# Top-2 experts of a decoder step: tokens fetched by indirect DMA in place of one-hot gathers

## Chip, cores and metric

The kernel runs on one core of a Trainium2 chip. The metric is the device time of one execution in microseconds (us), the median of several runs. The trace comes from one further, profiled execution.

## The reference

A two-layer decoder trunk runs one inference step on 320 tokens (256 of a prompt, 8 sequences of 8) with 1024 channels, in float32. Both layers mix tokens (pooling, convolution, gated DeltaNet) and end in a feed-forward part; layer 0 has a dense one, layer 1 has 8 experts of width 1408, of which each token uses two. Only the experts are touched here:

```
vals, idx = lax.top_k(xt @ w_router + b_router, 2)
gate = sum(one_hot(idx, 8) * softmax(vals)[..., None], axis=1)
for e in range(8):
    out = out + gate[:, e:e+1] * ((silu(xt @ wg[e]) * (xt @ wu[e])) @ wd[e])
```

## The kernel before

Precision is float32 throughout. Every matrix is split into a high part (`mh`, `xeh`, `hTh`: a copy rounded to the format TensorE multiplies) and a low part (`ml`, `xel`, `hTl`: the value minus its high part), and each product is three matmuls, low x high, high x low, high x high (L1340 to L1342, in `wide`).

**The expert stage** starts behind the router. A token's slot in its expert (`posm`) makes one-hot matrices `Pm` (`places`, VectorE, L1957), 128 slots for each expert. The first pair of experts gets its tokens by `gather`: matmuls of the token rows `xth` and `xtl` with `Pm` (L1288). Then the eight experts follow one another. An expert has 27 rows of weights, `MN`: 8 gate rows and 8 up rows of 1408 columns (704 KB each, 9 matmuls each, into banks 0 to 2 and 3 to 5), and 11 down rows of 1024 columns (512 KB, 6 matmuls, banks 6 and 7).

**A row's path**: SP loads it into one of 7 buffers `mraw` (L517), once the low part of the row 7 before is made; ScalarE copies it to one of 4 buffers `mh` (`mhead`, L901), once TensorE is through with the row 4 before; the low part `ml` is made by GpSimd for the rows in `MPOOL` (7 of the 27, L583) and by VectorE for the rest (`mlo`, L1938); then TensorE multiplies it. VectorE and ScalarE run step by step in the order of rows: step n makes row n + 3, and other work is placed behind it.

**Between up and down** ScalarE has put silu of the gate banks into `sg1`; VectorE multiplies it with banks 3 to 5 (L2012), TensorE transposes the product (11 transposes, L1389), ScalarE takes the high part `hTh` (L961) and VectorE the low part `hTl` (L2018). In experts 0 to 5 TensorE also gathers here for the expert two further on: 24 matmuls with `Pm`, half ahead of the transposes and half behind them (`gather_next`, for `xth` in even experts, for `xtl` in odd ones). Each gather ends in copies out of the banks on ScalarE and VectorE (`gathered`).

**Other work.** Even experts make the gates by slot (`slots`, L1306) and, from expert 2 on, add the pair before to the result: `scatter` (L1329, L1330) behind rows 3 to 10, whose banks VectorE adds to `acc` (`add`, L1977). Odd experts transpose `Pm` (`places_turned`). At an expert's end `y_head` (ScalarE) and `y_rest` (VectorE, L1972) take the down banks.

Of the kernel before, what the change touches and what calls it, by code (L numbers as in the profile page):

```python
# [54 lines left out]
MPOOL = (3, 6, 9, 12, 19, 22, 25)  # L55
# [11 lines left out]
for _n, _w in (("ident", 128), ("ones", 1), ("pick", 15), ("cum_p", 128), ("blk_p", 128), ("strict_p", 128), ("cum_s", 64),  # L67
               ("blk_s", 64), ("strict_s", 64), ("ind_p", 8), ("ind_s", 8), ("lev", 6 * 128), ("lev0t", 128),
               ("invcnt", 64), ("before", 64),
               ("upto", 128), ("slot", 128)):  # L70
    CON[_n] = (_at, _w)
    _at += _w
# [3 lines left out]
def build(nc, io):  # L76
# [8 lines left out]
    with ctx:  # L85
# [6 lines left out]
        def lay(at, *plan):  # L92
# [10 lines left out]
         gslot, flag, warm, TOP) = lay(  # L103
# [12 lines left out]
            ("gslot", [128, NE], f32), ("flag", [128, 1], mybir.dt.int32), ("warm", [1, 1], f32))  # L116
# [49 lines left out]
        assert E7 <= XS + 2 * size([1, KT, T]) + 12 * UNIT * 4  # L166

# [65 lines left out]
        m_hi, m_lop, m_lod, m_done = sem("m_hi"), sem("m_lop"), sem("m_lod"), sem("m_done")  # L233
        m_p, m_pt, m_ptc, m_gs = sem("m_p"), sem("m_pt"), sem("m_ptc"), sem("m_gs")
# [110 lines left out]
        def pooled(n):  # L345
            return n % MN in MPOOL

        def m_rest(n):

            mine = pooled(n)  # L350
            return (m_lop if mine else m_lod), sum(pooled(v) == mine for v in range(n + 1))
# [177 lines left out]
        def _(pool):  # L529
# [26 lines left out]

            pool.sem_inc(f_lo, 5)
            for l in range(DEPTH):
# [18 lines left out]
                else:  # L577
                    for n in range(MT):
                        if not pooled(n):
                            continue  # L580
                        w = mwidth(n % MN)
                        pool.wait_ge(m_hi, n + 1)
                        pool.tensor_tensor(ml[:, n % MS, 0:w], mraw[:, n % MRAW, 0:w],  # L583
                                           mh[:, n % MS, 0:w].bitcast(f32), ALU.subtract).then_inc(m_lop, 1)
# [8 lines left out]
        def _(act):  # L593
# [309 lines left out]
            def experts():  # L903
# [17 lines left out]
                def gathered(e, n):  # L921

                    act.wait_ge(m_g, 8 + 4 * e + n + 1)
                    dst = xel[:, 2 * n:2 * n + 2, :] if e % 2 else xeh[:, (e // 2 + 1) % 2, 2 * n:2 * n + 2, :]
                    act.activation(dst, PS[(7, 6, 0, 1)[n]][:, :].rearrange("p (k n) -> p k n", k=2), ACT.Copy)\
                        .then_inc(m_xea, 1)
# [10 lines left out]
                for n in range(MT):  # L937
# [3 lines left out]
                    if n and n + 3 < MT:  # L941
                        mhead(n + 3)
                    if i == MG - 1:
# [4 lines left out]
                    if i == 4 and e % 2 == 0:  # L948
                        act.wait_ge(m_gs, e // 2 + 1)
                        act.activation(gslot[:, e:e + 2], PS[3][:, 0:2], ACT.Copy).then_inc(m_ptc, 1)  # L950
# [4 lines left out]
                    if i == MG + MU - 1:  # L955
                        if e < NE - 2:
                            gathered(e, 0)
# [6 lines left out]
                        if e < NE - 2:  # L964
                            gathered(e, 2)
# [51 lines left out]
        def _(pe):  # L1017
# [253 lines left out]
            def experts():  # L1271
# [21 lines left out]
                def gather_next(e, n):  # L1293

                    gather(PS[(7, 6, 0, 1)[n]], xtl if e % 2 else xth, e // 2 + 1, n)

                def slots(e):

                    if e:
                        pe.wait_ge(m_tlo, 3 * e)  # L1300
                    pe.wait_ge(m_p, e + 2)
                    if not e:
                        pe.wait_ge(gate_made, 1)
                    for j in range(2):
                        for t in range(3):
                            ins = pe.matmul(PS[3][:, j:j + 1], Pm[0:rows(t), e // 2 % 2, t, j, :].bitcast(f32),  # L1306
                                            gate[0:rows(t), t, e + j:e + j + 1], start=(t == 0), stop=(t == 2))
                    ins.then_inc(m_gs, 1)
# [10 lines left out]
                def scatter(pair, m):  # L1319

                    if m == 0:
                        pe.wait_ge(m_ylo, 4 * pair + 4)
                        pe.wait_ge(m_ptc, 3 * pair + 3)
# [20 lines left out]

                pe.wait_ge(m_p, 2)
# [5 lines left out]
                for e in range(NE):  # L1351
# [7 lines left out]
                    def fed(k):  # L1359
                        return xeh[:, e // 2 % 2, k, h], xel[:, k, h]  # L1360

                    for k in range(8 + SCAT):
                        if k < MG:
                            wide(e * MN + k, PS[0:3], FUNIT, *fed(k), k == 0, k == MG - 1)
                        else:
                            if k == MG:
                                pe.wait_ge(m_ptc, 3 * (e // 2) + (3 if e % 2 else 1))
                            wide(e * MN + k, PS[3:6], FUNIT, *fed(k - MG), k == MG, False)
                        if k == 2:
                            if e % 2:  # L1370
                                places_turned(e)
                            else:
                                slots(e)
# [3 lines left out]
                    for k in range(SCAT, MU):  # L1377
                        wide(e * MN + MG + k, PS[3:6], FUNIT, *fed(k), False, k == MU - 1)

                    if e < NE - 2:  # L1380
                        pe.wait_ge(m_p, 2 * (e // 2) + 4)
                        pe.wait_ge(m_ylo, 2 * e)
                        pe.wait_ge(m_acc, 8 * (e // 2))
                        gather_next(e, 0)
                        gather_next(e, 1)
                    for c in range(3):
                        pe.wait_ge(m_h, e * 3 + (c + 1))
# [4 lines left out]
                    if e < NE - 2:  # L1392
                        pe.wait_ge(m_silu, e * 3 + 3)
                        gather_next(e, 2)
                        gather_next(e, 3)
                        pe.wait_ge(m_xea, XA0 + 2 * e + 1)
                        pe.wait_ge(m_xev, XV0 + 2 * e + 1)
                    else:
                        pe.wait_ge(m_ylo, 2 * e)
                        pe.wait_ge(m_acc, 8 * (e // 2))  # L1400
# [61 lines left out]
        def _(dve):  # L1462
# [470 lines left out]
            def mlo(n):  # L1933
                if pooled(n):
                    return
# [3 lines left out]
                                  mh[:, n % MS, 0:w].bitcast(f32), ALU.subtract).then_inc(m_lod, 1)  # L1939

            def experts(l):
# [3 lines left out]
                dve.memset(gate[:, :, NE:], 0.0)  # L1945
# [15 lines left out]
                def gathered(e, n):  # L1961

                    dve.wait_ge(m_g, 8 + 4 * e + n + 1)
                    dst = xel[:, 2 * n:2 * n + 2, :] if e % 2 else xeh[:, (e // 2 + 1) % 2, 2 * n:2 * n + 2, :]
                    dve.tensor_copy(dst, PS[(7, 6, 0, 1)[n]][:, :].rearrange("p (k n) -> p k n", k=2)).then_inc(m_xev, 1)
# [28 lines left out]
                for n in range(MT):  # L1994
# [3 lines left out]
                    if n + 3 < MT:  # L1998
# [3 lines left out]
                    if i in (5, 7) and e % 2 == 0 and e < NE - 2:  # L2002
                        if e:
                            dve.wait_ge(m_pt, e // 2)
                        places(e + 2 + (i - 5) // 2)
                    if i == MG + MU - 1:
                        dve.wait_ge(m_silu, e * 3 + 3)
                        dve.wait_ge(m_done, e * MN + MG + MU)
                        for c in range(3):
                            w = min(512, FUNIT - 512 * c)  # L2010
                            s = slice(512 * c, 512 * c + w)
                            dve.tensor_tensor(sg1[:, s], sg1[:, s], PS[3 + c][:, 0:w], ALU.mult).then_inc(m_h, 1)  # L2012
                        if e < NE - 2:
                            gathered(e, 1)
                        for c in range(3):
                            k = min(4, FT - 4 * c)
# [4 lines left out]
                        if e < NE - 2:  # L2021
                            gathered(e, 3)
# [72 lines left out]
def _constants():  # L2095
# [22 lines left out]
    put("upto", (i <= j).astype(np.float32))  # L2118
# [102 lines left out]
```

## Time and profile before

| | |
|---|---|
| median of 3 runs | 1652.11 us (1652.07 to 1652.57) |
| profiled execution | 1651.5 us, its span 1649.7 us |
| mean granted TensorE clock | 0.948 of 2.4 GHz |
| busy over the span | TensorE 92%, VectorE 65%, ScalarE 52%, GpSimd 34% |
| expert loop | from 1166.95 us to about 1617 us of the span |

The span reaches from the first to the last instruction; the time of an execution is 1.8 us longer. A busy share is an average over stages that have different limits. Only the last third of the span, the experts, is touched by the change.

### The profile page before, as it was taken

What the parts mean: (1) busy time and instruction counts of PE and PEld (TensorE: products, weight loads), DVE (VectorE), ACT (ScalarE), POOL (GpSimd) and SP (SyncE); (2) the same over time, 40 slices, a digit from 0 to 9 for tenths busy, and PEclk for the clock granted to TensorE, in tenths of its full rate; (3) what the DMA queues carried; (4) which work ended last, traced back from release to release, by engine and by line L of the source; (5) the groups of instructions that cost most, each with busy time, mean ns of one, the idle gap of its engine ahead of it and who ended that gap; (6) DMA issues with size and microseconds to landing.
All of it is one profiled execution on the core that took longest, in us unless ns stands there. A gap on an engine that the chain in (4) does not pass through costs nothing. (4 is left out here: it accounts for less than half of the span.)

```text
span 1649.7 us, 23014 instructions
## 1 busy us (share of the span) xinstructions
PE 1520.7 (92%) x8707; PEld 1339.8 (81%) x8707; DVE 1077.6 (65%) x1546; ACT 853.0 (52%) x1472; POOL 555.4 (34%) x336
## 2 busy tenths in 40 slices
PE   7999799999799999799998998996999999999995
PEld 6789799787699999678898988973788888888774
DVE  6779786658611011467887855777477877787784
ACT  4656555532433233355565635313566676576673
POOL 0036543000376567300555520010233343343342
PEclk9999899989899999999998998897799999999998
DMA  6322124312355455053322333125387987798780
GB/s 245 128 77 92 63 77 133 128 52 96 128 165 167 118 152 166 1 182 103 103 78 77 100 118 120 55 80 206 126 302 284 330 314 289 256 358 319 266 328 33
DMA packets 57523, 264.66 MB, mean 160 GB/s; under 512 B 9024, under 2 KB 9664, under 8 KB 48448
## 3 DMA queue, kind: packets, MB, share of 16 engines
q1 hardware_dynamic: 57408, 263.11, 45.9%
q8 instruction: 74, 1.21, 0.3%
q14 instruction: 41, 0.34, 0.1%
HBM read 254.54 MB, written 8.54 MB: 159 GB/s over the span
## 5 line engine op out<-in xcount | busy, mean ns | idle before, releaser
L1020 PE MATMUL ps<-Xh,Wl 128*128 128x320 f32 x976 | 332.0, 340 | 26.2 <-DVE Wl L1816 14.6
L1938 DVE TENSOR_TENSOR ml<-mraw,mh 128x1408 fp32r<-128x1408 f32 (+1 forms) x160 | 291.4, 1854 | 75.9 <-ACT mh L901 75.9
L901 ACT ACTIVATE mh<-mraw 128x1408 fp32r<-128x1408 f32 (+1 forms) x216 | 268.0, 1253 | 112.9 <-PE ps L1342 110.9
L1021 PE MATMUL ps<-Xl,Wh 128*128 128x320 f32 x976 | 312.9, 321 | 0.0
L1022 PE MATMUL ps<-Xh,Wh 128*128 128x320 f32 x976 | 312.7, 320 | 0.0
L555 POOL TENSOR_TENSOR cacc<-cacc,G 128x320 f32<-128x320 f32 x180 | 192.5, 1069 | 350.4 <-ACT G L681 334.3
L583 POOL TENSOR_TENSOR ml<-mraw,mh 128x1408 fp32r<-128x1408 f32 (+1 forms) x56 | 178.7, 3192 | 320.3 <-ACT mh L901 320.3
L1020 PEld LDWEIGHTS ps<-Xh,Wl 128*128 128x128 f32 x976 | 193.9, 199 | 50.4 <-issue 29.2
L1816 DVE TENSOR_TENSOR Wl<-raw,Wh 128x1024 fp32r<-128x1024 f32 x138 | 174.9, 1268 | 75.9 <-ACT Wh L610 74.9
L1021 PEld LDWEIGHTS ps<-Xl,Wh 128*128 128x128 f32 x976 | 194.4, 199 | 0.3
L1022 PEld LDWEIGHTS ps<-Xh,Wh 128*128 128x128 f32 x976 | 193.6, 198 | 0.0
L535 POOL TENSOR_TENSOR fl<-fraw,fh 128x1024 fp32r<-128x1024 f32 (+1 forms) x60 | 158.6, 2649 | 88.4 <-ACT fh L848 88.4
L610 ACT ACTIVATE Wh<-raw 128x1024 fp32r<-128x1024 f32 x138 | 144.9, 1052 | 46.0 <-PE ps L1022 37.7
L1340 PE MATMUL ps<-mh,xel 128*128 128x512 f32 (+1 forms) x384 | 147.0, 383 | 1.9 <-issue 0.8
L1341 PE MATMUL ps<-ml,xeh 128*128 128x512 f32 (+1 forms) x384 | 145.1, 378 | 0.0
L1342 PE MATMUL ps<-mh,xeh 128*128 128x512 f32 (+1 forms) x384 | 145.0, 378 | 0.0
L848 ACT ACTIVATE fh<-fraw 128x1024 fp32r<-128x1024 f32 (+1 forms) x60 | 68.4, 1146 | 127.3 <-PE ps L1022 127.3
L1020 PE MATMUL ps<-Xh,fl 128*128 128x320 f32 x352 | 110.4, 314 | 9.3 <-DVE Xl L1616 7.6
L1021 PE MATMUL ps<-Xl,fh 128*128 128x320 f32 x352 | 109.1, 310 | 0.5 <-issue 0.5
L1022 PE MATMUL ps<-Xh,fh 128*128 128x320 f32 x352 | 109.1, 310 | 0.0
L1877 DVE TENSOR_TENSOR hf<-sg,ps 128x320 f32<-128x320 f32 x22 | 10.7, 488 | 131.3 <-PE ps L1022 130.9
L680 ACT ACTIVATE G<-cxp,par 128x256 f32<-128x256 f32 x180 | 90.5, 503 | 1.5 <-ACTq L688 1.2
(336 smaller groups left out, 2953.4 us busy)
## 6 DMA issues: line engine op xcount, KB each, us to landing
mraw<-w_moe SPq DMA_DIRECT2D x128, 704.0 KB, 6.7
raw<-w_mix SPq DMA_DIRECT2D x68, 1024.0 KB, 4.9
mraw<-w_moe SPq DMA_DIRECT2D x88, 512.0 KB, 4.7
fraw<-w_ffn SPq DMA_DIRECT2D x44, 512.0 KB, 3.5
fraw<-w_ffn SPq DMA_DIRECT2D x16, 704.0 KB, 4.0
Ss<-st_delta SPq DMA_DIRECT2D x2, 2048.0 KB, 9.4
o_delta_s<-Ss SPq DMA_DIRECT2D x8, 512.0 KB, 2.6
X<-x SPq DMA_DIRECT2D x2, 640.0 KB, 5.6
```

The costliest lines, as they stand in the source:

```text
L535: pool.tensor_tensor(fl[:, i % 3, 0:w], fraw[:, i % 5, 0:w], fh[:, i % 3, 0:w].bitcast(f32), ALU.subtract).then_inc(f_lo, 1)
L555: pool.tensor_tensor(cacc[:, i, :], cacc[:, i, :], G[:, 20 + n % 4, :], ALU.add).then_inc(tap_added, 1)
L583: pool.tensor_tensor(ml[:, n % MS, 0:w], mraw[:, n % MRAW, 0:w], mh[:, n % MS, 0:w].bitcast(f32), ALU.subtract).then_inc(m_lop, 1)
L901: act.activation(mh[:, n % MS, 0:w], mraw[:, n % MRAW, 0:w], ACT.Copy).then_inc(m_hi, 1)
L1020: pe.matmul(out, wl, xh, start=start, stop=False)
L1021: pe.matmul(out, wh, xl, start=False, stop=False)
L1022: return pe.matmul(out, wh, xh, start=False, stop=stop)
L1340: pe.matmul(o, xl, mh[:, n % MS, s], start=first, stop=False)
L1341: pe.matmul(o, xh, ml[:, n % MS, s], start=False, stop=False)
L1342: ins = pe.matmul(o, xh, mh[:, n % MS, s], start=False, stop=last)
L1816: dve.tensor_tensor(Wl[:, n % 3, :], raw[:, b % 3, u % 2, :], Wh[:, n % 3, :].bitcast(f32), ALU.subtract).then_inc(w_lo, 1)
L1938: dve.tensor_tensor(ml[:, n % MS, 0:w], mraw[:, n % MRAW, 0:w], mh[:, n % MS, 0:w].bitcast(f32), ALU.subtract).then_inc(m_lod, 1)
```

## The change

Only the first pair of experts is still gathered with one-hot matmuls. For the others GpSimd adds high and low token rows up again, writes them to a DRAM tensor `x_tok` (row 0 is zero, row 1 + t is token t), and fetches 128 rows for each expert by indirect DMA into `xg`. The row numbers come out of `slots`, which multiplies `Pm` with two columns now, the gate and the token's number (`tok`). TensorE turns the fetched rows (`turn_next`, 8 transposes an expert), ScalarE and VectorE split them (`turned`). `slots` of the pair p + 1 runs behind row 6 of the even expert of pair p. The last two up rows are multiplied bank by bank (`last_up`), with a semaphore for each bank. All low parts are made on VectorE; GpSimd makes none.

```
-MPOOL = (3, 6, 9, 12, 19, 22, 25)
...
+            def token_rows():
+                pool.wait_ge(m_g, 8)
+                pool.memset(xg[64:65, 2, :], 0.0).then_inc(tok_zero, 1)
...
+                for t in range(3):
+                    r = rows(t)
+                    pool.tensor_tensor(xs[0:r, t, :], xtl[0:r, t, :].bitcast(f32), xth[0:r, t, :].bitcast(f32),
+                                       ALU.add).then_inc(tok_sum, 1)
+                pool.dma_start(x_tok[0:1, :], xg[64:65, 2, :]).then_inc(tok_out, 16)
...
+                pool.wait_ge(tok_out, 64)
+            def fetch(pair):
+                pool.wait_ge(m_row, pair)
+                if pair > 1:
+                    pool.wait_ge(m_g, 8 + 2 * (2 * pair - 2))
+                for j in range(2):
+                    pool.indirect_dma_start(xg[:, j, :], None, x_tok[:, :],
+                                            bass.IndirectOffsetOnAxis(ap=row[:, 2 * pair + j:2 * pair + j + 1], axis=0))\
+                        .then_inc(xg_in[j], 16)
...
+                def turned(e, n):
+                    act.wait_ge(m_g, 8 + 2 * e + n + 1)
+                    act.activation(xeh[:, 0, 4 * n:4 * n + 4, CAP * (e % 2):CAP * (e % 2) + CAP],
+                                   PS[n][:, :].rearrange("p (k n) -> p k n", k=4), ACT.Copy).then_inc(m_xea, 1)
...
+                def last_up(e, rows_, xs):
+                    for k in rows_:
+                        pe.wait_ge(*m_rest(e * MN + MG + k))
+                    for c in range(3):
...
+                            if c == 2:
+                                ins.then_inc(m_done, 1)
+                        if c < 2:
+                            ins.then_inc(m_up, 1)
...
+                            elif k == MG and e < NE - 2:
+                                pe.wait_ge(m_gsc, e // 2 + 2)
+                                pe.wait_ge(m_row, e // 2 + 1)
...
+                        if k == 6 and e % 2 == 0 and e < NE - 2:
+                            slots(e, e // 2 + 1)
...
-                    if e < NE - 2:
...
-                        gather_next(e, 0)
-                        gather_next(e, 1)
                     for c in range(3):
+                        if c == 2 and e < NE - 2:
+                            pe.wait_ge(m_silu, e * 3 + 3)
+                            pe.wait_ge(xg_in[e % 2], 16 * (e // 2 + 1))
+                            turn_next(e, 0)
                         pe.wait_ge(m_h, e * 3 + (c + 1))
...
                     if e < NE - 2:
-                        pe.wait_ge(m_silu, e * 3 + 3)
-                        gather_next(e, 2)
-                        gather_next(e, 3)
...
+                        turn_next(e, 1)
...
-                    if n + 3 < MT:
+                    if n + 3 < MT and i != MG + MU - 1:
                         mlo(n + 3)
...
+                    if i == 7 and e % 2 == 0 and e < NE - 2:
+                        slot_rows(e // 2 + 1)
...
                         for c in range(3):
+                            if c == 1:
+                                mlo(n + 3)
                             k = min(4, FT - 4 * c)
                             dve.wait_ge(m_thi, e * 3 + (c + 1))
...
                         if e < NE - 2:
-                            gathered(e, 3)
+                            turned(e, 0)
+                            turned(e, 1)
```

## Rows read from the trace of the kernel before

**Rows 1.** Busy time by stretch, an odd and an even expert: us, then engines.

```profile
core 0: us, PE busy (x) PEld busy (x) DVE busy (x) ACT busy (x) POOL busy (x), PEclk, DMA share, GB/s
...
1226.00:1281.00 55.00, 54.92 (x253) 44.44 (x252) 44.15 (x31) 38.96 (x40) 22.91 (x7) 1.00 0.85 315
1281.00:1340.00 59.00, 59.00 (x288) 49.42 (x287) 47.73 (x45) 38.06 (x38) 22.21 (x7) 1.00 0.80 290
```

**Rows 2.** Timeline of TensorE, expert 1 from row 11 on.

```profile
1247.88 0.39 PE L1340 MATMUL ps<-mh,xel 128*128 128x512 f32 x1
...
1252.07 0.40 PE L1340 MATMUL ps<-mh,xel 128*128 128x512 f32 x1
...
1257.84 2.93 PE L1288 MATMUL ps<-Pm,xtl 128*128 128x256 f32 x12
1260.70 1.42 PE L1389 MATMUL ps<-con,sg 128*128 128x128 f32 x11
1261.88 3.02 PE L1288 MATMUL ps<-Pm,xtl 128*128 128x256 f32 x12
1264.83 0.50 PE L1340 MATMUL ps<-mh,hTl 128*128 128x512 f32 x1
...
1280.40 0.39 PE L1340 MATMUL ps<-mh,xel 128*128 128x512 f32 x1
```

**Rows 3.** Timeline of TensorE, expert 6: last up matmul, first down matmul.

```profile
1546.51 0.34 PE L1342 MATMUL ps<-mh,xeh 128*128 128x384 f32 x1
...
1550.27 0.47 PE L1340 MATMUL ps<-mh,hTl 128*128 128x512 f32 x1 [0.66 <-DVE hTl L2018]
```

**Rows 4.** Timeline of VectorE: start of the stage, and expert 2.

```profile
1142.39 3.87 DVE L1957 TENSOR_SCALAR Pm<-con,posm 128x128 fp32r<-128x128 f32 x6
...
1302.47 0.67 DVE L1957 TENSOR_SCALAR Pm<-con,posm 128x128 fp32r<-128x128 f32 x3
...
1309.57 1.61 DVE L1938 TENSOR_TENSOR ml<-mraw,mh 128x1408 fp32r<-128x1408 f32 x1
...
1318.14 1.74 DVE L2012 TENSOR_TENSOR sg<-sg,ps 128x512 f32<-128x512 f32 x3
```

**Rows 5.** Timeline of GpSimd: start of the stage, and expert 1.

```profile
1142.06 3.15 POOL L583 TENSOR_TENSOR ml<-mraw,mh 128x1408 fp32r<-128x1408 f32 x1 [26.87 <-ACT mh L901]
...
1233.04 4.70 POOL L583 TENSOR_TENSOR ml<-mraw,mh 128x1408 fp32r<-128x1408 f32 x1 [1.42 <-ACT mh L901]
```

**Rows 6.** Timeline of TensorE: first gather of the stage.

```profile
1146.32 9.94 PE L1288 MATMUL ps<-Pm,xth 128*128 128x256 f32 x24 [5.88 <-DVE Pm L1957]
```

**Rows 7.** Timeline of ScalarE, expert 1: the copy released by the end of row 12.

```profile
1252.33 1.07 ACT L901 ACTIVATE mh<-mraw 128x1024 fp32r<-128x1024 f32 x1 [0.89 <-PE ps L1342]
```

**Rows 8.** Groups by line and shape, 1166.5 to 1617: busy us, mean ns.

```profile
L1938 DVE TENSOR_TENSOR ml<-mraw,mh 128x1408 fp32r<-128x1408 f32 x93 | 192.8, 2105 | 31.6 <-ACT mh L901 31.6
L901 ACT ACTIVATE mh<-mraw 128x1408 fp32r<-128x1408 f32 x124 | 169.0, 1385 | 65.1 <-PE ps L1342 63.2 <-DMA mraw<-w_moe 0.9
...
L1938 DVE TENSOR_TENSOR ml<-mraw,mh 128x1024 fp32r<-128x1024 f32 x64 | 94.9, 1501 | 43.5 <-ACT mh L901 43.5
...
L1977 DVE TENSOR_TENSOR acc<-acc,ps 128x320 f32<-128x320 f32 x24 | 11.5, 479 | 6.9 <-PE ps L1330 6.9
...
L1972 DVE SCALAR_TENSOR_TENSOR yl<-ps,gslot,yh 128x512 fp32r<-128x512 f32 x14 | 9.8, 739 | 0.0
...
L961 ACT ACTIVATE hTh<-ps 128x512 fp32r<-128x512 f32 x16 | 8.9, 597 | 14.1 <-PE ps L1389 14.1
```

**Rows 9.** Timeline of TensorE, expert 2: a scatter behind row 3, then row 4.

```profile
1289.77 0.31 PE L1329 MATMUL ps<-PT,yl 128*128 128x320 f32 x1
...
1290.35 0.39 PE L1340 MATMUL ps<-mh,xel 128*128 128x512 f32 x1
```

**Rows 10.** Loads of L517, 1220 to 1340: time from issue to landing.

```profile
DMA to landing us min/median/max: 3.4/6.0/8.8
```

**Rows 11.** Busy time by stretch, 5 us inside expert 1.

```profile
1231.00:1236.00 5.00, 5.00 (x25) 3.95 (x24) 3.64 (x2) 2.73 (x4) 3.58 (x2) 1.00 1.02 419
```

**Rows 12.** Busy time by stretch, 2 us ahead of the first gather.

```profile
1142.00:1144.00 2.00, 0.00 (x0) 0.00 (x0) 1.93 (x4) 0.00 (x0) 1.94 (x1) 0.50 0.91 313
```

More of the change, by code:

```diff
@@ L69 @@
                ("invcnt", 64), ("before", 64),
[L70 removed]
+               ("upto", 128), ("slot", 128), ("tok", 3)):
     CON[_n] = (_at, _w)
@@ L343, in mwidth @@
             return FUNIT if i < MG + MU else D
-        def pooled(n):
-            return n % MN in MPOOL
         def m_rest(n):
-            mine = pooled(n)
-            return (m_lop if mine else m_lod), sum(pooled(v) == mine for v in range(n + 1))
+            return m_lo, n + 1
         def m_loaded(n):
@@ L577, in _ @@
                 else:
[L578 to L584, printed above, removed]
+                    token_rows()
+                    for pair in range(1, NE // 2):
+                        fetch(pair)
                     sums(m_acc, 4 * NE - 8, asum, KT - 1)
@@ L1291, in gather, with turn_next, slots @@
                     ins.then_inc(m_g, 1)
[L1293 to L1297 removed]
+                def turn_next(e, n):
+                    for k in range(4):
+                        f = 512 * n + 128 * k
+                        ins = pe.transpose(PS[n][:, 128 * k:128 * k + 128], xg[:, e % 2, f:f + 128], C("ident"))
+                    ins.then_inc(m_g, 1)
+                def slots(e, p):
                     if e:
                         pe.wait_ge(m_tlo, 3 * e)
[L1301 to L1302 removed]
+                    pe.wait_ge(m_p, 2 * p + 2)
+                    if p < 2:
                         pe.wait_ge(gate_made, 1)
+                    if p == 1:
+                        pe.wait_ge(m_gsc, 1)
                     for j in range(2):
+                        i = 2 * p + j
                         for t in range(3):
[L1306 to L1307 removed]
+                            ins = pe.matmul(PS[3][:, 2 * j:2 * j + 2], Pm[0:rows(t), p % 2, t, j, :].bitcast(f32),
+                                            gate[0:rows(t), t, i:NE + 1:NE - i], start=(t == 0), stop=(t == 2))
                     ins.then_inc(m_gs, 1)
@@ L1959, in places, with turned, slot_rows @@
                     ins.then_inc(m_p, 1)
[L1961 to L1965, printed above, removed]
+                def turned(e, n):
+                    dve.wait_ge(m_xea, XA0 + 2 * e + n + 1)
+                    own = slice(CAP * (e % 2), CAP * (e % 2) + CAP)
+                    dve.tensor_tensor(xel[:, 4 * n:4 * n + 4, own], PS[n][:, :].rearrange("p (k n) -> p k n", k=4),
+                                      xeh[:, 0, 4 * n:4 * n + 4, own].bitcast(f32), ALU.subtract).then_inc(m_xev, 1)
+                def slot_rows(p):
+                    dve.wait_ge(m_gsc, p + 1)
+                    dve.tensor_copy(row[:, 2 * p:2 * p + 2], PS[3][:, 1:4:2]).then_inc(m_row, 1)
                 def y_rest(e):
```

93 lines of the change are left out of this document (50 added, 43 removed).

## Prediction

> **What bounds the kernel now.** I read the page first for the stage that the change touches, then the chain of waits: from 1166 us to 1617 us it is TensorE alone that ends last. The busy times by stretch say so plainly: in an odd expert TensorE works 54.92 of 55.00 us, in an even one 59.00 of 59.00, both at the full granted clock, while VectorE has 44 to 48 us of work and GpSimd 22 to 23 [rows 1]. So what TensorE no longer issues shortens the kernel, as long as nobody makes it wait instead. I then read TensorE's timeline for the length of each piece. Three up rows run from 1252.07 to 1257.84, 1.92 us each; the two rows before them took 4.19 us instead of 3.85, a delay of 0.34 us where a low part from GpSimd came late. From the end of the up rows to the first down matmul it is 1257.84 to 1264.83, 6.99 us: twelve gather matmuls of 2.86, eleven transposes of 1.18 (0.107 each), twelve gather matmuls of 2.95. The eleven down rows take 15.57, 1.42 each [rows 2]. In expert 6, which gathers nothing, the last up matmul starts at 1546.51 (0.17 long by the pace of its neighbours), the first down matmul at 1550.27: 3.59 us, which TensorE spends mostly waiting for the product and its split [rows 3].
>
> **Start of the stage.** `places` for the first pair makes six small matrices in 3.87 us, where three take 0.67 elsewhere [rows 4]. A GpSimd low part runs from 1142.06 to 1145.21, over just this time [rows 5], and TensorE's first gather waits for the matrices, idle for 5.88 us [rows 6]. GpSimd no longer makes that low part, so six should take 2 x 0.67 = 1.34: **2.5 us** gained.
>
> **The block between up and down, experts 0 to 5.** I count from E, the end of the up rows. TensorE's own work is 8 transposes of the first two banks (0.86), 4 of the fetched tokens (1.29), 3 of the third bank, 4 more of tokens: 19 x 0.107 = 2.03. The other condition for the down rows is the first low part `hTl`. A ScalarE copy starts 0.26 after the row that releases it (1252.33 against 1252.07 [rows 2, 7]). The copy of row 18 waits for row 14, whose last third now ends 3 x 0.17 = 0.52 ahead of E, so it runs from E - 0.26 to E + 0.81; then `hTh` takes 0.60 [rows 8], and VectorE's `hTl` about 0.65 (three pieces of that kind take 1.74 [rows 4]): with the passing on about E + 2.2. The products are ready in time: banks 3 and 4 are full at E - 2.44 and E - 1.04. So 2.2 in place of 6.99, 4.79 x 6 = **28.7 us** gained. Experts 6 and 7 go from 3.59 to 2.2 as well, **2.8 us** together.
>
> **Low parts.** With GpSimd out, the 0.34 us of each of four odd experts goes too: **1.4 us**. A low part on VectorE takes 2.1 us on average [rows 8] but 1.61 where GpSimd rests [rows 4]; for 1024 columns I scale that to 1.2. VectorE then has in an odd expert 16 x 1.61 + 11 x 1.2 = 39.0, products 1.74, `hTl` about as much, two `turned` 1.3, `y_rest` 2 x 0.74: 45.3 us. An even one adds eight `add` of 0.48 and two `places` of 0.67: 50.4. TensorE needs 16 x 1.92 + 2.2 + 15.6 = 48.6 and, with eight scatters of 0.58 [rows 9], 53.2, before its small work. The extra seven low parts cost nothing, hidden under TensorE; what they cost without that cover is a rival below. The two last up rows now wait for both low parts at the start of the first: from the end of row 11, 0.26 + 1.39 + 1.61 = 3.26 against 3.84 of cover, so nothing; an overrun would be paid by all eight experts.
>
> **New waits.** (a) VectorE's order behind the block: `hTl` until 2.1, low part of row 18 until 3.3, two more `hTl` until 4.4, two `turned` until 5.8, low part of row 19 until 7.0. TensorE has done rows 16 to 18 at 2.2 + 3 x 1.41 = 6.4, so it waits about 0.65, six times: **3.9 us** lost. Rows 20 on are late by less than TensorE's pace gives back. (b) In experts 2 and 4 row 8 waits for `slot_rows`, which stands on VectorE behind the `add` of the scatter just issued: 0.26 + 0.48 + about 0.2 = 0.95, twice: **1.9 us** lost. In expert 0 there is no scatter, and row 7 covers it. Queued behind `slot_rows` are only low parts with 2 us to spare.
>
> **The fetch.** No row shows an indirect DMA. From below it is free. From above: a GpSimd instruction took 4.70 beside VectorE instead of some 3.15 [rows 5], a load landed 8.8 us after issue at worst [rows 10]; 13.5 us together, an estimate. The cover is the eight up rows of the even expert, 15.4 us, and 1.7 of scatters in experts 2 and 4. I take nothing; if it is late, three experts pay. The sums and writes of `x_tok` (three GpSimd adds, at most 14 us by the 4.70, and 8.8 to land) lie under the first 15 rows of expert 0, some 30 us. SP's queue is not passed by anything. An expert's weights are 16 x 704 KB + 11 x 512 KB = 17.3 MB, in 50 us 346 GB/s, and 1 MB more for a pair's tokens; the queues moved 419 where they were full [rows 11].
>
> **The sum.** 2.5 + 28.7 + 2.8 + 1.4 - 3.9 - 1.9 = 29.6 us. The profiled execution took 1651.5, so 1621.9; the median of the runs lies 0.6 above it: **1622.5 us**. Its own range takes the waits at 0 to twice their size and the block at 2.0 to 2.7: 1615 to 1630. Waiting at neither place gives 1616.7.
>
> **Rivals.** (1) *The order behind the block costs more.* Copies and splits of the turned tokens stand between `hTl` and row 19 on both engines; if each of the four pieces adds another 0.5 us of passing on, row 19 is 2 us later in six experts: 1622.5 + 12 = 1634.5. For it speaks that VectorE is 85 to 95% full; against it that ScalarE ends its part at 3.7, well ahead of VectorE. Chance 0.13.
> (2) *VectorE becomes the bound*, the case on the other side. If its low parts keep their means of 2.105 and 1.501 [rows 8], an odd expert has 16 x 0.495 + 11 x 0.3 = 11.2 us more, 56.5, an even one 61.6: 118.1 for a pair against 114 now [rows 1], so 4 x 4.1 - 2.5 = 14 slower: 1666. It decides from a mean of about 1.78 over all low parts on. Against it: the 1.61 where GpSimd rests, and that GpSimd now rests nearly always. Chance 0.04.
> (3) *The fetched rows come late.* If GpSimd takes 4.70 for a fetch and the rows land twice as late as the worst load, 4.70 + 17.6 = 22.3 us, TensorE stands 6.9 us at the end of expert 0 and 5.2 at the ends of 2 and 4: 1622.5 + 17 = 1640. From about 26 us on nothing of the gain is left. For it speaks only the 4.70 beside 3.15 [rows 5]; the cover is over 15 us. Chance 0.08. The Trainium skill has a rule for this ("SBUF — State Buffer", section "SBUF: two separate sides", the note on DVE and DMA): descriptors of a GpSimd DMA are written by GpSimd, which can be shut out of a port shared with VectorE, and a DMA of 620 ns then took 3100. The rule names VectorE's two-port modes, in which low parts (two inputs) don't run; five times the landing of a load at its median (6.0 [rows 10]) would be an estimate of 30 us, past this case, and 1663 (14.6 + 2 x 12.9 later) in place of 1622.5, where the sum without the rule has no wait. No run shows it yet.
> (4) *The clock stays up.* The granted clock is 0.50 while TensorE waits for the first matrices [rows 12], and the first 24 gather matmuls take 9.94, 0.41 each [rows 6], against 0.24 at full clock [rows 2]. If the shorter wait kept it up, 48 x 0.17 = 8 us and some 2.5 of the first rows more are gained: 1612. Against it: it is down at 1142, before the gather could start even now. Chance 0.06.
>
> **How the numbers follow.** The forecast has 0.69, the rivals 0.13, 0.04, 0.08 and 0.06. The range takes the forecast, the clock and the order behind the block: 1611 to 1637, and leaves out late fetches and VectorE as the bound, 0.12, with some of the tails. A change of 0.2% (3.3 us) is about what a measurement can tell from none. Faster are the forecast, (1), (4) and nearly all of (3): 0.93; within 0.2%: 0.02; slower 0.05, from (2) and a fetch of more than 27 us.
>
> **What would show it.** Right: twelve gather matmuls gone from TensorE's line in each of six experts' two places, 19 transposes in a row, blocks of about 2.2 us; low parts of 1.61 and 1.2; the first gather at about 1143.8; a gap of 0.65 before row 19 and 0.95 before row 8 of experts 2 and 4; odd experts of about 50, even ones of about 55 us. Wrong: gaps released by VectorE's low parts all along the rows (2), by the fetch's queue ahead of the token transposes (3), or a pace of 0.24 in the first gather (4).

## Result and the profile after

The changed kernel takes **1616.56 us** (median of 4 runs, 1615.73 to 1618.42) against 1652.34 for the kernel before in the same runs: a ratio of 0.9782, with a 95% interval of 0.9767 to 0.9798, or 35.8 us less. In a later set of runs (run 8 below) it took 1619.74 against 1650.96, 31.2 us less. The forecast was 1622.5 in a range of 1611 to 1637. The profiled execution took 1615.73, its span 1613.9.

Busy time by stretch, an odd expert (1) and an even one (2) of the changed kernel, from the first gate row of one to that of the next:

```profile
core 0: us, PE busy (x) PEld busy (x) DVE busy (x) ACT busy (x) POOL busy (x), PEclk, DMA share, GB/s
...
1218.10:1267.90 49.80, 49.77 (x236) 41.47 (x235) 44.03 (x38) 38.70 (x40) 0.00 (x0) 1.00 0.91 350
1267.90:1323.80 55.90, 55.13 (x274) 47.14 (x273) 48.67 (x53) 38.39 (x39) 1.88 (x2) 1.00 0.89 328
```

They answer to [rows 1]: TensorE is still what ends last, GpSimd has nothing left in them but the two fetches, and VectorE, with 44 of 50 us, is close behind but not the bound.

TensorE's timeline of the changed kernel at the place of [rows 2], expert 1 between up and down:

```profile
1249.85 0.34 PE L1384 MATMUL ps<-mh,xeh 128*128 128x384 f32 x1
1250.02 1.03 PE L1437 MATMUL ps<-con,sg 128*128 128x128 f32 x8
1250.89 0.60 PE L1318 MATMUL ps<-con,xg 128*128 128x128 f32 x4
1251.33 0.49 PE L1437 MATMUL ps<-con,sg 128*128 128x128 f32 x3
1251.66 0.60 PE L1318 MATMUL ps<-con,xg 128*128 128x128 f32 x4
1252.28 0.47 PE L1367 MATMUL ps<-mh,hTl 128*128 128x512 f32 x1
```

Nineteen transposes in a row, no gather, and 2.26 us from 1250.02 to 1252.28 where there were 6.99. Expert 6 turns no tokens, has eleven transposes, and takes as long, since TensorE waits there for `hTl`:

```profile
1517.08 0.47 PE L1367 MATMUL ps<-mh,hTl 128*128 128x512 f32 x1 [0.90 <-DVE hTl L2070]
```

So the first low part of the product ends last in the block, and the token transposes lie in its shadow. VectorE's timeline, expert 1 again:

```profile
1248.68 1.28 DVE L2064 TENSOR_TENSOR sg<-sg,ps 128x512 f32<-128x512 f32 x2
1250.22 0.56 DVE L2064 TENSOR_TENSOR sg<-sg,ps 128x384 f32<-128x384 f32 x1 [0.27 <-PE ps L1384]
1251.34 0.69 DVE L2070 TENSOR_TENSOR hTl<-ps,hTh 128x512 fp32r<-128x512 f32 x1 [0.56 <-ACT hTh L981]
1251.94 1.22 DVE L1979 TENSOR_TENSOR ml<-mraw,mh 128x1024 fp32r<-128x1024 f32 x1
1253.08 1.15 DVE L2070 TENSOR_TENSOR hTl<-ps,hTh 128x512 fp32r<-128x512 f32 x2
1254.14 1.28 DVE L2006 TENSOR_TENSOR xel<-ps,xeh 128x512 fp32r<-128x512 f32 x2
1255.34 6.89 DVE L1979 TENSOR_TENSOR ml<-mraw,mh 128x1024 fp32r<-128x1024 f32 x6
```

The first two products are made while the last up row runs. Everything behind them follows in the forecast order, closer together than forecast: the low part of row 19 (first of the last line) begins 5.3 after the end of the up rows and ends at about 6.5, not 7.0.

Start of the stage: VectorE's matrices and TensorE's first gather, against [rows 4] and [rows 6].

```profile
1141.09 1.26 DVE L1998 TENSOR_SCALAR Pm<-con,posm 128x128 fp32r<-128x128 f32 x6
```

```profile
1142.40 9.94 PE L1309 MATMUL ps<-Pm,xth 128*128 128x256 f32 x24 [3.29 <-DVE Pm L1998]
```

1.26 us instead of 3.87, as forecast. The gather still takes 0.41 per matmul, at a granted clock of 0.50 as in [rows 12] (columns as above):

```profile
1142.00:1144.00 2.00, 1.60 (x4) 1.15 (x5) 2.00 (x5) 0.00 (x0) 0.00 (x0) 0.50 0.42 173
```

Groups by line and shape over the stage, against [rows 8]:

```profile
L1979 DVE TENSOR_TENSOR ml<-mraw,mh 128x1408 fp32r<-128x1408 f32 x125 | 204.6, 1671 | 31.6 <-ACT mh L923 31.1
L923 ACT ACTIVATE mh<-mraw 128x1408 fp32r<-128x1408 f32 x124 | 169.9, 1384 | 62.0 <-PE ps L1369 55.7 <-DMA mraw<-w_moe 5.3
L1979 DVE TENSOR_TENSOR ml<-mraw,mh 128x1024 fp32r<-128x1024 f32 x88 | 104.7, 1221 | 8.6 <-ACT mh L923 8.2
```

Low parts take 1.67 and 1.22 us (2.105 and 1.501 before). ScalarE now waits 5.3 us for loads (0.9 before); none of it reaches TensorE. The fetch on GpSimd, expert 0, and how long its transfers take (page, DMA issues, median time to landing):

```profile
1163.29 10.97 POOL L564 TENSOR_TENSOR xs<-xtl,xth 128x1024 f32<-128x1024 f32 x3
...
1185.53 1.03 POOL L579 DMA_INDIRECT xg<-x_tok,row  x1 [8.95 <-DVE row L2012]
1186.87 0.96 POOL L579 DMA_INDIRECT xg<-x_tok,row  x1 [0.30 <-issue]
```

```profile
xg<-x_tok,row POOLq DMA_INDIRECT x6, 6.8
```

A fetch costs GpSimd 1 us and lands 6.8 later at the median. The first one lands 6.4 after its issue, at 1191.9, and TensorE turns its rows at 1201.1, 9 us later. The two new waits of TensorE, row 8 in expert 0 and in expert 2:

```profile
1183.80 0.34 PE L1369 MATMUL ps<-mh,xeh 128*128 128x384 f32 x1
1184.77 0.47 PE L1367 MATMUL ps<-mh,xel 128*128 128x512 f32 x1 [0.63 <-issue]
```

```profile
1287.76 0.31 PE L1357 MATMUL ps<-PT,yh 128*128 128x320 f32 x1
1288.76 0.47 PE L1367 MATMUL ps<-mh,xel 128*128 128x512 f32 x1 [0.70 <-issue]
```

By the pace of the rows, TensorE loses 0.80 in expert 0 and 0.85 in experts 2 and 4. The first was not forecast. VectorE and GpSimd in expert 0 say why:

```profile
1164.60 12.68 DVE L1979 TENSOR_TENSOR ml<-mraw,mh 128x1408 fp32r<-128x1408 f32 x4
...
1184.52 0.15 DVE L2012 CAST row<-ps 128x2 int32<-128x2 f32 x1
```

Four low parts take 12.68 us, 3.2 each, beside GpSimd's three sums of token rows (10.97 us in the same stretch). VectorE is behind by then, and makes the row numbers at 1184.52, half a microsecond after TensorE has finished row 7.

The lengths of the experts, from the first matmul of one to that of the next (expert 7: to the last low x high matmul of its last down row), worked out from TensorE's timeline, and their sum, which I call the stage below:

| expert | 0 | 1 | 2 | 3 | 4 | 5 | 6 | 7 | stage |
|---|---|---|---|---|---|---|---|---|---|
| before | 58.61 | 54.84 | 59.72 | 54.83 | 59.72 | 54.85 | 56.30 | 50.6 | 449.5 |
| after | 55.06 | 49.81 | 55.94 | 49.80 | 55.94 | 49.80 | 53.16 | 49.0 | 418.5 |

### The profile page after: what moved, and what is told of

It reads as the page before. It is cut to its first block and busy times, and to the rows that moved or that the text cites. A ratio compares the mean times of both kernels' runs of the same rounds, so it can differ in the third digit from the quotient of the medians.

```text
span 1613.9 us, 22849 instructions
## 1 busy us (share of the span) xinstructions
PE 1487.7 (92%) x8611; PEld 1320.4 (82%) x8611; DVE 1089.6 (68%) x1605; ACT 851.3 (53%) x1472; POOL 397.2 (25%) x294
## 5 line engine op out<-in xcount | busy, mean ns | idle before, releaser
L1979 DVE TENSOR_TENSOR ml<-mraw,mh 128x1408 fp32r<-128x1408 f32 (+1 forms) x216 | 313.9, 1487 | 41.0 <-ACT mh L923 40.1
L1367 PE MATMUL ps<-mh,xel 128*128 128x512 f32 x336 | 128.1, 381 | 2.9 <-issue 2.9
L1368 PE MATMUL ps<-ml,xeh 128*128 128x512 f32 x336 | 127.2, 379 | 0.0
L1369 PE MATMUL ps<-mh,xeh 128*128 128x512 f32 x336 | 127.1, 378 | 0.0
L1041 PEld LDWEIGHTS ps<-Xh,fl 128*128 128x128 f32 x352 | 66.5, 189 | 12.0 <-POOL fl L535 8.5
```

The lines of the kernel that those rows point to most:

```text
L1041: pe.matmul(out, wl, xh, start=start, stop=False)
L1367: pe.matmul(o, xl, mh[:, n % MS, s], start=first, stop=False)
L1368: pe.matmul(o, xh, ml[:, n % MS, s], start=False, stop=False)
L1369: ins = pe.matmul(o, xh, mh[:, n % MS, s], start=False, stop=last)
L1979: dve.tensor_tensor(ml[:, n % MS, 0:w], mraw[:, n % MRAW, 0:w], mh[:, n % MS, 0:w].bitcast(f32), ALU.subtract).then_inc(m_lo, 1)
```

## Experiments

Kernels that differ in nothing ahead of the stage began it at 1162.0 to 1166.1 us (the two profiles of the changed kernel and those of runs 3 to 5), and two sets of runs of the changed kernel had medians 3.2 us apart (1616.56 and 1619.74). So small effects are read from the length of the stage in the profile, which agreed to 0.1 us in the two profiles of the changed kernel, and the times are given beside it. Differences from the kernel before are worked out from the ratios in runs 1 and 2, and from the medians elsewhere unless said otherwise.

**1. Only the low parts, in the kernel before.**

```
         def pooled(n):
-            return n % MN in MPOOL
+            return False
```

> The kernel before, all low parts on VectorE. Theory (the gathers are the bulk of the gain): only the earlier first gather (2.6 us) and the low parts of GpSimd that came late (about 2) are gained, 1652.3 - 4.6 = 1647.7 us. Rival A (VectorE becomes the bound while it also empties the gathers): 1655 us or more. Rival B (the low parts are the bulk): 1635 us or less.

Measured: 1646.89 us, ratio 0.9968 (0.9956 to 0.998): 5.3 faster. The stage is 447.7, 1.8 shorter. It would be 3.2 shorter but for the first down rows of expert 6, which lose 1.4 at a granted clock of 0.50 (from 1543.4 to 1546.7); why it fell there is not shown. The matrices at its start take 1.26 us, and the low parts (VectorE's groups of this kernel) are as short as in the changed kernel:

```profile
L1938 DVE TENSOR_TENSOR ml<-mraw,mh 128x1408 fp32r<-128x1408 f32 x125 | 198.5, 1622 | 37.4 <-ACT mh L901 37.3
L1938 DVE TENSOR_TENSOR ml<-mraw,mh 128x1024 fp32r<-128x1024 f32 x88 | 107.7, 1224 | 27.7 <-ACT mh L901 27.6
```

So the whole move is free for VectorE and worth a little by itself; the case in which VectorE becomes the bound is out. Experts 6 and 7, which gather nothing, keep their block of 3.58 and 3.59 us: faster low parts alone don't shorten it.

**2. Only the gathers, in the kernel before**: one matmul for each gather in the loop instead of six.

```
-                    for k in range(2):
+                    for k in range(2 if pair == 0 else 1):
...
-                        for t in range(3):
+                        for t in range(3 if pair == 0 else 1):
```

> The kernel before with one matmul in place of six in each gather inside the experts (most tokens of experts 2 to 7 are left out, all copies stay). Theory: the block between up and down falls from 6.99 us not to the 2.26 of the change but only to about 3.7, as in expert 6, since product and split then end last: 6 x 3.3 = 20 us, 1632 us. Rival (the block is as long as its matmuls): 6.99 - 4.9 = 2.1, so 29 us, 1623 us.

Measured: 1634.25, ratio 0.9877 (0.9856 to 0.9899), 20.3 less (18.1 by the medians); the stage is 432.2, 17.3 shorter. TensorE in expert 1:

```profile
1256.50 0.39 PE L1288 MATMUL ps<-Pm,xtl 128*128 128x256 f32 x2
1257.81 1.61 PE L1389 MATMUL ps<-con,sg 128*128 128x128 f32 x11 [0.92 <-DVE sg L2012]
```

With a sixth of the gathers left, the block is 3.78, not 2.26: TensorE stands 0.92 for the products, because VectorE makes them only behind a low part and all three behind the last row. The gathers had covered that. Six blocks are 19.2 us shorter; expert 3 gives back 1.4, where TensorE waits for a low part of VectorE that ran beside GpSimd's (three in 9.61 us). The rest of the block needs another edit.

**3. The changed kernel without the bank-by-bank up rows.**

```
-                    for k in range(SCAT, MU - 2):
-                        wide(e * MN + MG + k, PS[3:6], FUNIT, *fed(k), False, False)
-                    last_up(e, (MU - 2, MU - 1), fed)
+                    for k in range(SCAT, MU):
+                        wide(e * MN + MG + k, PS[3:6], FUNIT, *fed(k), False, k == MU - 1)
...
-                            if c < 2:
-                                dve.wait_ge(m_up, 2 * e + c + 1)
-                            else:
-                                dve.wait_ge(m_done, e * MN + MG + MU)
+                            dve.wait_ge(m_done, e * MN + MG + MU)
```

> The changed kernel with the last two up rows row by row again, one signal for all three banks. Theory: the first product starts 0.3 us behind the rows in place of ahead of them, the block goes from 2.26 to about 3.0 us in all eight experts, 1616.6 + 6 = 1622.6 us. Rival (the transposes of the fetched tokens cover the products as the gathers did): 1616.6 us, no change.

Measured: 1627.59, ratio 0.9836 (0.9813 to 0.9859), some 9 us over the changed kernel by the ratios, where I had expected 6; the stage is 426.7, 8.2 longer. TensorE in expert 1:

```profile
1253.47 0.34 PE L1369 MATMUL ps<-mh,xeh 128*128 128x384 f32 x1
1254.66 1.25 PE L1436 MATMUL ps<-con,sg 128*128 128x128 f32 x8 [0.85 <-DVE sg L2060]
...
1256.94 0.47 PE L1367 MATMUL ps<-mh,hTl 128*128 128x512 f32 x1
```

The block is 3.3 us, of which 0.85 is a wait for the first product that the changed kernel doesn't have: about 1.03 more in each of eight experts.

**4. The changed kernel without sums, DRAM copy and fetch.**

```
-                    token_rows()
-                    for pair in range(1, NE // 2):
-                        fetch(pair)
...
-                            pe.wait_ge(xg_in[e % 2], 16 * (e // 2 + 1))
```

> The changed kernel without the sums, the DRAM copy and the six fetches; TensorE turns whatever lies in the buffer (experts 2 to 7 get wrong tokens). Theory: the fetches are covered, only the wait of 0.8 us before row 8 of expert 0 goes, for which VectorE was held up beside GpSimd's sums: 1615.8 us. Rival (the fetches' 4.5 MB delay the weights): 4.5 MB at 419 GB/s are 10.6 us, 1606 us.

Measured: 1618.66, ratio 0.9793 (0.9776 to 0.981), which can't be told from the changed kernel. The stage is 417.7, 0.8 shorter, and the 0.8 is row 8 of expert 0, whose wait is gone. So the fetch itself is free, as forecast, and what comes with it costs 0.8; the low parts of 3.2 us beside the sums say that this goes through VectorE.

**5. Row numbers ahead of the addition of the scatter.**

```
+                    if i == 7 and e % 2 == 0 and e < NE - 2:
+                        slot_rows(e // 2 + 1)
                     if SCAT <= i < SCAT + 8 and e and e % 2 == 0:
                         add(e // 2 - 1, i - SCAT)
...
-                    if i == 7 and e % 2 == 0 and e < NE - 2:
-                        slot_rows(e // 2 + 1)
```

> The changed kernel, with the making of the row numbers (slot_rows) put ahead of the add of the scatter at the same step of VectorE. My theory of the waits of row 8: in experts 2 and 4 the 0.85 to 0.95 us come from the add that stands ahead on VectorE, so both waits shrink to under 0.4; expert 0, where there is no add, keeps its 0.8. Gain 1.0 to 1.9 us: 1614.7 to 1615.6, hard to tell in the time, plain in the timeline of TensorE. Rival: the wait is set by the way from the small matmuls through ScalarE's copy of the gates, whatever VectorE does first; then all three waits stay as they are, 1616.6.

Measured: 1615.78 (1614.99 to 1617.87), ratio 0.9786 (0.977 to 0.9801); the changed kernel beside it on the same chip took 1619.74 (run 8). By time that is between 0.8 and 4 us; the timeline is exact. The stage is 416.6, 1.9 shorter. Experts 2 and 4 take 55.0 instead of 55.94, with no gap ahead of row 8, and expert 0 keeps its own (0.57 of idle time). The addition ahead on VectorE was the cause of the two waits.

**6. The same kernel with TensorE kept busy ahead of the first gather.**

```
+                pe.wait_ge(m_hi, 1)
+                for _ in range(13):
+                    pe.matmul(PS[6][:, 0:512], mh[:, 0, 512:640], mh[:, 0, 0:512], start=True, stop=True)
                 pe.wait_ge(m_p, 2)
```

> The changed kernel, with 13 more matmuls of 512 columns on TensorE ahead of its wait for the first matrices (they multiply weights into a bank that nothing reads). Theory A, the clock is down in the first gather because TensorE idles about 3.3 us ahead of it: the clock stays at 1.00, the 48 gather matmuls take 0.24 each instead of 0.41 and the first rows start at full clock, 8 to 10 us less: 1606 to 1609. Theory B, the clock falls in the gather for something in the gather itself or in what comes after: the gather starts at full clock at best and falls to 0.50 within it, or the added matmuls themselves run at 0.50, 13 x 0.43 = 5.6 us against 3.3 of idle time: 1615 to 1619.

Measured: 1612.91 (1612.15 to 1613.53), ratio 0.9767 (0.9752 to 0.9783): 3.7 to 6.8 us under the changed kernel. TensorE's timeline and the busy times by stretch (columns as above):

```profile
1142.22 3.24 PE L1392 MATMUL ps<-mh 128*128 128x512 f32 x13
1145.62 6.02 PE L1309 MATMUL ps<-Pm,xth 128*128 128x256 f32 x24 [0.17 <-DVE Pm L2001]
1151.57 8.34 PE L1309 MATMUL ps<-Pm,xtl 128*128 128x256 f32 x24
1160.74 0.77 PE L1367 MATMUL ps<-mh,xel 128*128 128x512 f32 x1 [0.83 <-issue]
```

```profile
1147.00:1152.00 5.00, 5.00 (x21) 3.18 (x20) 2.78 (x8) 2.11 (x4) 0.00 (x0) 1.00 0.00 0
1152.00:1157.00 5.00, 5.00 (x17) 3.22 (x16) 0.00 (x0) 1.47 (x3) 0.00 (x0) 0.70 0.00 0
1157.00:1163.00 6.00, 5.17 (x12) 3.56 (x13) 3.71 (x4) 0.00 (x0) 2.95 (x2) 0.50 0.01 3
```

Half of each theory. The first gather runs at the full 2.4 GHz, 6.02 us for 9.94, and the way from the first gather to the first row is 15.1 us instead of 20.6. But in the second gather the clock falls to 1.2 GHz although TensorE is busy all the time, and the first rows start slowly as before. So what TensorE does ahead of the gather decides the clock of the first gather. That it is the idle time there which lowers it is not shown: in run 11, with the same 13 matmuls, the clock fell to 0.50 while TensorE was busy, and was back at 1.00 for the first gather.

```profile
1141.40:1144.60 3.20, 3.20 (x9) 2.42 (x8) 3.03 (x14) 0.53 (x1) 0.00 (x0) 0.50 0.73 228
```

```profile
1145.14 5.91 PE L1309 MATMUL ps<-Pm,xth 128*128 128x256 f32 x24
```

What lowers it in the second gather was not tried.

**7. Seven low parts of each expert back on GpSimd**, in the changed kernel (six in expert 0).

```
+MPOOL = (3, 6, 9, 12, 19, 22, 25)
...
+        def pooled(n):
+            return n % MN in MPOOL and n != 6
...
+                        if pooled(n):
...
+                            pool.tensor_tensor(ml[:, n % MS, 0:w], mraw[:, n % MRAW, 0:w],
+                                               mh[:, n % MS, 0:w].bitcast(f32), ALU.subtract).then_inc(m_lop, 1)
...
+                        if i == 9 and e % 2 == 0 and e < NE - 2:
+                            fetch(e // 2 + 1)
```

> The changed kernel, with seven low parts of each expert given back to GpSimd (six in expert 0), the fetch placed behind row 9's place on GpSimd. Low parts on VectorE then take about 2.1 and 1.5 us again, odd experts have some 0.3 of TensorE waiting for GpSimd, and the first matrices take 3.9 instead of 1.3 us. Theory: 2.6 at the start, 1.4 in odd experts and up to 1 for a slower order behind the block: 4 to 5 us more than the changed kernel, 1620.5 to 1621.5. Rival, GpSimd's low parts and the fetch get in each other's way (the writing of the descriptors late, rows of tokens late): TensorE waits for tokens ahead of the token transposes, 1626 or more. Other rival: nothing measurable, 1616.6.

Measured: 1642.6 (1633.03 to 1645.09), ratio 0.9947 (0.9929 to 0.9965). I had expected 4 to 5 us more than the changed kernel, and it is 23 to 26. My rival's number, 1626 or more, holds, but not its cause: TensorE never waits for token rows. The profiled execution was the fastest of the six (1633.03); its stage is 433.7, 15.3 longer.

**8. The changed kernel once more**, beside runs 5 to 7.

> The changed kernel once more, on the same chip as the three others, so that their times can be set against it: 1614 to 1618.

Measured: 1619.74 (1616.96 to 1624.02), ratio 0.9814 (0.9796 to 0.9833), above what I expected; stage 418.4.

**9. Run 7 once more, and 10. run 7 without sums, DRAM copy and fetch** (its other lines as in run 4), to find where the 23 us are.

> The run with seven low parts on GpSimd once more, beside the one without the fetch. Its times lay from 1633 to 1645, its profiled execution was the fastest of them. By its profile the stage is 15 us longer than the changed kernel's, 16 to 19 us with its start: 1633 to 1637; by its median 1642. If the median holds, the profile should show where the rest comes from.

> The run with seven low parts on GpSimd, without the sums, the DRAM copy and the fetch (experts 2 to 7 are computed with other tokens). Theory now: the loss of that run is in the low parts themselves, which take turns on GpSimd and VectorE and come late for TensorE where nothing covers them any more; the fetch has only the wait of row 8 (2.2 us in expert 0, 0.5 in expert 2). So 3 to 4 us come back of the 23: 1636 to 1640 by the times, and a stage of about 430 in the profile in place of 433.7. Rival: GpSimd's own order (a fetch between two low parts) makes the delays; then nearly all comes back: a stage of 418 to 420, 1619 to 1622.

Measured: 1643.99 (1643.35 to 1646.67) for run 9, ratio 0.9953 (0.9938 to 0.9969), and 1638.44 (1633.06 to 1642.22) for run 10, ratio 0.9909 (0.9888 to 0.9931). Without the fetch most of the loss stays, so GpSimd's order is not its main cause. The stage of run 10 is 437.1 and not 430, mostly for a loss in expert 4 that is explained below. The lengths of the experts:

| expert | 0 | 1 | 2 | 3 | 4 | 5 | 6 | stage |
|---|---|---|---|---|---|---|---|---|
| changed kernel (8) | 55.07 | 49.80 | 55.94 | 49.81 | 55.93 | 49.81 | 53.16 | 418.4 |
| split (7) | 58.73 | 51.71 | 57.71 | 51.73 | 58.28 | 51.74 | 53.68 | 433.7 |
| split again (9) | 58.77 | 51.73 | 62.77 | 51.73 | 61.38 | 51.72 | 53.69 | 441.9 |
| split, no fetch (10) | 56.70 | 51.73 | 58.55 | 51.72 | 62.91 | 51.74 | 53.67 | 437.1 |

Three things add up. First, late low parts: in each odd expert up to 5 they cost 1.9 us (0.8 at three down rows, 0.35 at row 12, 0.8 at the last two up rows), and even experts and expert 7 pay part of it. Secondly, row 8 of expert 0: it waits 2.69 us in run 7 for its row numbers, 2.1 more than in the changed kernel. Thirdly, losses of 5 us and more against the changed kernel in expert 2 or 4, in one run and not in the next (experts 2 and 4 of run 9, expert 4 of run 10). VectorE, GpSimd and TensorE of run 9, expert 2:

```profile
1291.42 3.63 DVE L2016 TENSOR_SCALAR Pm<-con,posm 128x128 fp32r<-128x128 f32 x3
```

```profile
1291.79 3.18 POOL L616 TENSOR_TENSOR ml<-mraw,mh 128x1408 fp32r<-128x1408 f32 x1 [2.70 <-ACT mh L939]
```

```profile
1292.40 0.34 PE L1385 MATMUL ps<-mh,xeh 128*128 128x384 f32 x1
1295.20 2.96 PE L1349 MATMUL ps<-gate,Pm 128*128 128x2 f32 x12 [2.46 <-DVE Pm L2016]
```

The matrices had begun 0.37 us before a GpSimd low part, and stretched over the whole of it, 3.63 us for 0.67. `slots` needs them at once now, so TensorE stood 2.46 us, went on at half its clock (0.50 from 1295 to 1300; 2.96 for 12 matmuls that take 1.66), and lost 5.6 us in rows 6 and 7. TensorE stands 2.46 us at the same place in expert 4 of runs 9 and 10. In run 7 the same three matrices fell earlier and the GpSimd instruction gave way:

```profile
1290.35 0.67 DVE L2016 TENSOR_SCALAR Pm<-con,posm 128x128 fp32r<-128x128 f32 x3
```

```profile
1290.72 4.92 POOL L616 TENSOR_TENSOR ml<-mraw,mh 128x1408 fp32r<-128x1408 f32 x1 [2.70 <-ACT mh L939]
```

A few tenths of a microsecond in the order of two engines decide over 5 us. The stages of runs 7 and 9 differ by 8.2 us for this, of 10.3 between their two profiled executions (1633.03 and 1643.35). That the other executions from 1633 to 1645 differ for the same reason is likely, but they have no profile.

**11. Both edits that worked, 5 and 6 together.**

> The changed kernel with both edits that worked one by one: the row numbers made ahead of the add, and the 13 matmuls ahead of the first gather. If the two gains add (1.7 us in the timeline of TensorE from the first, 4 to 7 us from the second), 1610 to 1612; rival: the earlier rows run into VectorE or into the loads of weights and only the second gain is left, 1613.

Measured: **1611.62** (1609.8 to 1615.6), ratio 0.976 (0.9746 to 0.9773), the lowest median here. Its stage is 416.5, that of run 5. Against run 6 alone (0.9767) the times can't tell it apart. Against the kernel before it is faster; against the changed kernel its times are lower than all of both sets (1615.73 and up), but no changed kernel ran beside it, and the intervals of the ratios touch that of the first set.

## Why the prediction was right

The forecast had the mechanism and most of its sizes. Its terms against the two profiles:

| term | forecast | measured |
|---|---|---|
| matrices at the start | 2.5 | 2.6 |
| block, experts 0 to 5 | 28.7 | 28.3 (6 x (6.98 - 2.26)) |
| block, experts 6 and 7 | 2.8 | 2.7 |
| GpSimd low parts late | 1.4 | 2.9 |
| wait at row 19 | -3.9 | -1.0 |
| wait at row 8 | -1.9 | -2.7 |
| clock in the first rows | 0 | 0.4 |
| behind the last down row | 0 | 0.8 |
| work ahead of the stage | 0 | 1.3 |
| sum | 29.6 | 35.3 of 35.8 |

The last two terms, 0.8 and 1.3, are no effect of the change (below). Of the 35.8 between these two profiles, 33 to 34 are thus the change's; the forecast was 4 short of that, mostly at row 19 and in the late low parts.

**The block** came out to a tenth of a microsecond, and for the reason given: the second condition, `hTl` 2.2 us behind E, the end of the up rows, ends last (the wait in expert 6 above). Runs 2 and 3 show that it takes both edits: cutting the gathers alone leaves 3.78, the fetch without the bank-by-bank rows 3.3. The forecast gave the sum to the block as one and did not say how it divides. Of 31.0 us in eight blocks, 19.2 go with the gathers (run 2) and 8.2 with the bank-by-bank rows (run 3); the other 3.6 lie between the block of run 2 (or of experts 6 and 7) and that of run 3, and no run divides them further. One difference is that the products stand behind a low part in the one and not in the other. VectorE's faster low parts alone gave nothing here (run 1, experts 6 and 7).

**Low parts late** was too small: besides the four odd experts, expert 0 lost 1.0 at one row, and each expert 0.06 at its end. Run 1 has all of these gone.

**Row 19** is the largest miss. VectorE's pieces behind the block follow one another without a pause, since ScalarE is ahead by then (its part of `turned` ends at 1253.32, VectorE's begins at 1254.14), and each is shorter than forecast. They begin 1.92, 3.06, 4.12 and 5.32 us behind E where the forecast had 2.1, 3.3, 4.4 and 5.8, the step of two `turned` (1.2 for 1.4) most of all. TensorE loses 0.16, six times, where 0.65 was forecast; the forecast's own figures, 7.0 and 6.43, give 0.57. The rival of a slower order behind the block had the sign wrong: the order costs less than the forecast, not more.

**Row 8** was right in experts 2 and 4, cause and size: run 5 removes exactly these two and shortens each expert by 0.94, for 0.95 forecast. For expert 0 the forecast said that row 7 covers it. It priced GpSimd's sums only as far as the fetch waits for them and not for what they do to VectorE beside them; that costs 0.8 us, and run 4 removes it. (The 2.7 of the table is 1.9 by run 5 and 0.8 by run 4.)

**VectorE as the bound** would have needed low parts of 1.78 us in the mean; they take 1.49 (1.67 and 1.22 over 125 and 88).

**The fetch** is free, as forecast, with the upper bound far off: 1.0 us of GpSimd and 6.8 to land, against the 13.5 allowed. The Trainium skill's rule against it ("SBUF — State Buffer", "SBUF: two separate sides": descriptors starved by VectorE) did not show here: GpSimd's instructions took 0.94 to 1.03 us, and TensorE never waits for the rows. But where I argued that low parts, with two inputs, are not of the kind that shuts GpSimd out, I was wrong; run 7 shows it below.

**The clock.** The rival of a clock that stays up was rightly held unlikely: the changed kernel's gather starts at 0.50 and is still at 0.41 a matmul at its end. Run 6 gets 5.5 of the 8 us that the rival gave for two gathers at full clock, since the second one falls back. What I left out is in the first rows: the second row of expert 0 takes 2.38 us for 2.81 before, since the clock is up earlier in it. From the last down row to the end it is 31.7 us instead of 32.5, and the last scatter starts at full clock (0.15 a matmul) and not at half (0.27). But in run 8, the same kernel, this stretch is 34.0 us and the scatter is at 0.27 throughout, so these 0.8 us are chance.

**Work ahead of the stage.** The first gather starts 3.9 us earlier (1142.40 against 1146.32 [rows 6]), 2.6 of it from the matrices. The other 1.3 come from before them and are no effect of the change: the start of the stage varies by 4 us from run to run.

**Its own range.** The forecast's rule, waits at twice their size and blocks of 2.7 us, gives 1632 at the top, not 1630 (1628.3 + 8 x 0.5). Nothing hangs on it here.

## What to carry to other kernels

What an edit is worth depends on what still stands in its place. Moving the low parts was worth 5 us in the kernel before, and undoing it cost 23 to 26 in the changed one. The same seven rows are late at more places there: in the kernel before, the down rows behind GpSimd's keep their pace of 1.40 but for 0.06 us at the end, and in run 7 three of them lose 0.8 together. I put that down to the long block, which gave the low parts a head start; no run shows it by itself. And the matrices are now needed at once: in run 7, expert 2, `slots` starts 0.5 us behind them. So price an edit at the kernel that will stand at the end, and try each edit both ways: alone in the old kernel, and left out of the new one.

When a busy stretch is cut between two dependent steps, look next at what it had covered; here it was the product, and only making it piece by piece under the row before turned 3.3 us into 2.26.

## What the hardware showed that was not expected

**VectorE and GpSimd take turns.** In run 7 a low part on GpSimd began at 1184.82 and one on VectorE at 1184.86:

```profile
1184.82 3.19 POOL L616 TENSOR_TENSOR ml<-mraw,mh 128x1408 fp32r<-128x1408 f32 x1 [7.26 <-ACT mh L939]
```

```profile
1184.86 4.63 DVE L1997 TENSOR_TENSOR ml<-mraw,mh 128x1408 fp32r<-128x1408 f32 x1 [2.01 <-ACT mh L939]
```

VectorE's takes 1.61 alone; 3.19 + 1.61 is 4.80, so it stood for nearly the whole of GpSimd's. With the other order (run 7, 1290.72) GpSimd's took 4.92. The Trainium skill has this rule ("SBUF — State Buffer", "SBUF: two separate sides"): the port that the two share is an exclusive lock for a whole instruction, held by whichever starts first, and an operation of VectorE with two inputs in SBUF meets it when GpSimd reads SBUF too. The trace agrees, and so do the 3.2 us of each low part beside the sums of token rows. The same holds for the fetch. In run 7 one was issued 0.08 us behind the start of a low part:

```profile
1189.77 1.62 DVE L1997 TENSOR_TENSOR ml<-mraw,mh 128x1408 fp32r<-128x1408 f32 x1 [0.21 <-ACT mh L939]
```

```profile
1189.85 2.47 POOL L586 DMA_INDIRECT xg<-x_tok,row  x1 [1.84 <-DVE row L2030]
```

It ends 0.93 us behind the low part's end, as if it had begun only there. Two more fetches began behind a low part, and both are long too: 1.99 us at 1299.11 in run 7, and 2.46 at 1190.90 in run 9. In the changed kernel, where each fetch begins first or alone, none takes over 1.03. The wait cost nothing: the rows landed 8 us before they were turned. The forecast had the turn-taking in its rows (4.70 for 3.15 [rows 5]) and took it for a longer duration, where it is a wait that falls on whichever engine comes second. Where it drew on the section above, it looked only at the two-port modes and passed over two inputs.

**The clock falls without idle time.** In run 6 it goes from 1.00 to 0.50 within the second gather, with TensorE busy for 5.00 of 5.00 us. In run 11 it is at 0.50 ahead of the first gather (3.20 of 3.20 us busy) and, after 1.00, again at the end of the second. Why is open.
